# Heads of 64 divided before their transposition and multiplied in pairs; the norm sum and one split moved in the FFNs

## What is computed

```python
def rms_norm(x, g):
    return x * lax.rsqrt(jnp.mean(x * x, axis=-1, keepdims=True) + EPS) * g

# pa: 8 heads of 64, causal with a slope on the distance
logit = einsum('bhqd,bhkd->bhqk', q, k) * scale - slopes * dist
a = einsum('bhqk,bhkd->bhqd', softmax(logit), v)

# hybrid layer: three branches of width 512
# mla: 8 heads, values of 64
o_mla = einsum('bhqk,bkhd->bqhd', softmax(s), v)
# diff: 4 heads of 128 with two maps each
o_diff = einsum('bhqk,bkhd->bqhd', p[:, 0] - lam * p[:, 1], v)
# window: 8 heads of 64, two key/value heads, a sink in the denominator
m = maximum(max(s, axis=-1, keepdims=True), sink)
e = exp(s - m)
p = e / (sum(e, axis=-1, keepdims=True) + exp(sink - m))
o_win = einsum('bhgqk,bkhd->bqhgd', p, v)
merged = gates[0] * (o_mla @ w_branch[0]) + gates[1] * (o_diff @ w_branch[1]) \
       + gates[2] * (o_win @ w_branch[2])

# causal FFN
u, g = split(causal_dwconv(rms_norm(x) @ w_in), 2)
x = x + (gelu(g) * u) @ w_out
# gated FFN
x = x + (gelu(depthwise_conv(h @ w_ffn_gate)) * (h @ w_ffn_up)) @ w_ffn_down
```

## Time and profile before

| | us |
|---|---|
| median of 3 executions | 1570.9 |
| lowest, highest | 1570.85, 1575.32 |
| profiled execution | 1571.56 |
| its span in the profile | 1569.7 |
| TensorE busy | 1541.5 |
| VectorE busy | 1144.7 |
| ScalarE busy | 910.6 |
| GpSimd busy | 156.7 |

### The profile page before, as it was taken

One profiled execution on the slowest core, in us unless ns is written; L12 is line 12 of the kernel. 1 busy time (PEld: TensorE's weight loads), 2 busy tenths in 40 slices (PEclk: granted clock), 3 DMA queues, 4 the chain that ended last, 5 costly groups with the idle time before them and its releaser, 6 DMA issues.

```text
span 1569.7 us, 30181 instructions
## 1 busy us (share of the span) xinstructions
PE 1541.5 (98%) x12792; PEld 1494.6 (95%) x12792; DVE 1144.7 (73%) x1382; ACT 910.6 (58%) x1213; POOL 156.7 (10%) x91
## 2 busy tenths in 40 slices
PE   7999999999999999999999999999999999999998
PEld 7899999999999999899899999999889899999998
DVE  6768777888988787778458875678778647776666
ACT  6566544698666565556465644456645555644444
POOL 0211211100011110000030100010000013011010
PEclk9999999999999999999999999999999999999999
DMA  9345555444546545423244555544542334455552
GB/s 317 126 146 184 198 191 181 164 167 150 180 166 214 187 161 200 150 97 119 85 165 162 188 190 185 188 162 162 183 140 91 120 99 160 173 200 202 176 187 77
DMA packets 38412, 258.73 MB, mean 165 GB/s; under 512 B 4768, under 2 KB 5408, under 8 KB 7840
## 3 DMA queue, kind: packets, MB, share of 16 engines
q1 hardware_dynamic: 37872, 255.33, 46.9%
q10 hardware_dynamic: 432, 1.84, 0.3%
HBM read 256.10 MB, written 1.05 MB: 164 GB/s over the span
## 4 chain that ended last, share of the span: by engine, by line
PE 79%; issue 8%; ACT 6%; DVE 5%; POOL 0%; DMA 0%; SPq 0%; POOLq 0%; ACTq 0%; DVEq 0%
PE bank L1710 24%; PE bank L1712 23%; PE bank L1711 23%; PE bank L2019 3%; PE bank L1972 3%; PE bank L1991 2%; ACT w_hi L483 2%; DVE w_lo L990 2%; PE bank L1942 1%; DVE h_lo L1005 1%; PE bank L1915 1%; ACT h_hi L503 1%; DVE qk L1106 1%; DVE x L1081 0%; POOL y_lo L1632 0%
## 5 line engine op out<-in xcount | busy, mean ns | idle before, releaser
L1710 PE MATMUL bank<-h_hi,w_hi 128*128 128x256 f32 x2640 | 751.9, 285 | 14.2 <-DVE h_lo L1005 9.4
L1711 PE MATMUL bank<-h_lo,w_hi 128*128 128x256 f32 x2640 | 742.0, 281 | 0.0
L1712 PE MATMUL bank<-h_hi,w_lo 128*128 128x256 f32 x2640 | 741.8, 281 | 0.0
L990 DVE TENSOR_TENSOR w_lo<-raw,w_hi 128x2048 fp32r<-128x2048 f32 x237 | 549.6, 2322 | 168.6 <-ACT w_hi L483 167.4
L483 ACT ACTIVATE w_hi<-raw 128x2048 fp32r<-128x2048 f32 x237 | 452.8, 1912 | 237.5 <-PE bank L1712 237.5
L1710 PEld LDWEIGHTS bank<-h_hi,w_hi 128*128 128x128 f32 x2640 | 497.7, 189 | 26.6 <-issue 20.9
L1712 PEld LDWEIGHTS bank<-h_hi,w_lo 128*128 128x128 f32 x2640 | 500.9, 190 | 0.0
L1711 PEld LDWEIGHTS bank<-h_lo,w_hi 128*128 128x128 f32 x2640 | 497.3, 188 | 0.3
L1710 PE MATMUL bank<-y_hi,w_hi 128*128 128x256 f32 x1040 | 294.4, 283 | 3.1 <-DVE y_lo L1447 1.4
L1712 PE MATMUL bank<-y_hi,w_lo 128*128 128x256 f32 x1040 | 291.6, 280 | 0.0
L1711 PE MATMUL bank<-y_lo,w_hi 128*128 128x256 f32 x1040 | 291.5, 280 | 0.0
(11 more groups left out here) (227 smaller groups left out, 1339.7 us busy)
## 6 DMA issues: line engine op xcount, KB each, us to landing
raw<-W SPq DMA_DIRECT2D x237, 1024.0 KB, 4.8
raw<-W SPq DMA_DIRECT2D x4, 512.0 KB, 7.4
wide<-RW ACTq DMA_DIRECT2D x1, 1280.0 KB, 6.9
x<-XT SPq DMA_DIRECT2D x4, 256.0 KB, 6.6
OUT<-x SPq DMA_DIRECT2D x4, 256.0 KB, 2.0
wide<-CON SPq DMA_DIRECT2D x1, 768.0 KB, 9.7
val<-PE_T ACTq DMA_DIRECT2D x2, 256.0 KB, 2.7
vec<-VEC SPq DMA_DIRECT2D x1, 390.0 KB, 4.6
```

What stands on the lines that cost most here:

```text
L990: V.tensor_tensor(w_lo[:, n0 % NW], raw[:, n0 % NRAW], w_hi[:, n0 % NW].bitcast(F32), ALU.subtract)\
L1710: T.matmul(out, w[0], a[0], start=start, stop=False, **kw)
L1711: T.matmul(out, w[0], a[1], start=False, stop=False, **kw)
L1712: return T.matmul(out, w[1], a[0], start=False, stop=stop, **kw)
```

## The change

It has three parts.

1. Heads of 64 (all of pa, the window and mla heads of hy). `divide`, new on VectorE, multiplies a map's exponentials in `lg` by the reciprocal of their sums (with the sink's term added first) and signals `norm_done`; `transposed` waits for that instead of `exp_done`. TensorE's `output_pair`, new, takes two maps at once: the values (64 columns) are stationary and 256 columns of `pt` move, one head into partitions 0 to 63 and one into 64 to 127 of the bank, so the result is already transposed. It stands at every second step, in place of `outputs` at every step. The transpositions of `ot` by TensorE and the division by VectorE's `outputs` go; ScalarE's `leave` copies the bank to its place. The window heads are taken in another order. In hy `leave(7)` stands directly behind the first sigmoid.
2. Causal FFNs: `normed` moves from behind the first unit's products to behind tile 0 of the second unit's.
3. Gated FFNs, first step: ScalarE's `after(u)` moves ahead of its activations on the products, VectorE's ahead of the wait for them and of the convolution.

```diff
-            for h in (0, 4, 1, 5, 2, 6, 3, 7):
+            for h in (0, 5, 1, 4, 2, 7, 3, 6):
...
-        TURNS = {"pa": {5: [0], 8: [1]}, "hy": {12: [0], 13: [1], 16: [2], 17: [3], 21: [4], 24: [5]}}
+        TURNS = {"pa": {}, "hy": {12: [0], 13: [1]}}
...
-                    if not late:
+                    if not late or not s0:
                         after(u, i)
...
                     ins.then_inc(sems["tu"], 1)
-                    if late:
+                    if late and s0:
                         after(u, i)
...
+            def leave(s, g):
+
+                gg = total(s, "ogroups") + g
+                act.wait_ge(sems["pv_done"], gg + 1)
+                nc.scalar.activation(ot_tiles(s, g if kind(s) == "pa" else g - 2), bank[2 + gg % 2][:], ACT.Copy)\
+                    .then_inc(sems["o_ev"], 1)
...
+                    if kind(s) == "hy" and i in (17, 21):
+                        for g in {17: (4, 5), 21: (6,)}[i]:
+                            leave(s, g)
...
                     nc.scalar.activation(g, g, ACT.Sigmoid).then_inc(sems["sig_done"], 1)
+                    if b == 0:
+                        leave(s, 7)
                     if b < 2:
                         branch_input(s, b + 2)
-                    if b == 0:
-                        turn(s, ("pair", 5))
...
-                    if not late and s0:
+                    if not late and s0 or not causal and not s0:
                         after(u, i)
 
                     dve.wait_ge(sems["tu"], done(1))
...
-                    if late or not s0:
+                    if late and s0 or causal and not s0:
                         after(u, i)
...
+            def divide(s, i):
+
+                m, a = att_maps(s)[i], 2 + i % 2
+                dve.wait_ge(sems["exp_done"], total(s, "maps") + i + 1)
+                z = sums[:, m["col"]]
+                if m["sink"] is not None:
+                    link(V.tensor_tensor(z, z, esink[:, m["sink"]], ALU.add))
+                link(V.reciprocal(rec[:, a], z))
+                for qt in range(2):
+                    p = lg[:, i % 2, qt * S:(qt + 1) * S]
+                    last = V.tensor_scalar(p, p, rec[:, a, qt:qt + 1], None, ALU.mult)
+                last.then_inc(sems["norm_done"], 1)
...
+                if kind(s) == "pa":
+                    divide(s, 0)
...
+                    if att_maps(s)[i]["w"] == 64 and att_maps(s)[i]["dist"]:
+                        divide(s, i)
                     if i + 1 < n:
                         logits(s, i + 1)
...
                     if i + 2 < n:
                         logits(s, i + 2)
+                        if att_maps(s)[i + 1]["w"] == 64:
+                            divide(s, i + 1)
+                            if not att_maps(s)[i + 2]["dist"]:
+                                divide(s, i + 2)
...
                     else:
                         first_unit(s, ba)
-                        if causal:
-                            normed(s)
...
                     column_tile(u + 1, 0, bb[:, 0:S])
-                    if not causal and s0 == 0:
+                    if s0 == 0:
                         normed(s)
-                        embedding_sum(s)
+                        if not causal:
+                            embedding_sum(s)
...
-                    pe.wait_ge(sems["exp_done"], total(s, "maps") + u[1] + 1)
+                    if att_maps(s)[u[1]]["w"] == 64:
+                        pe.wait_ge(sems["norm_done"], normed_no(s, u[1]))
+                    else:
+                        pe.wait_ge(sems["exp_done"], total(s, "maps") + u[1] + 1)
...
+            def output_pair(s, i):
...
+                output_bank(s, i)
+                output_bank(s, i + 1)
+                pe.wait_ge(sems["pt_ev"], use_no(s, ("map", i + 1)) + 1)
+                for kt in range(2):
+                    for e in (i, i + 1):
+                        m = att_maps(s)[e]
+                        a, r = m["slot"] // 2, 64 * (m["slot"] % 2)
+                        last = T.matmul(bank[2 + (total(s, "ogroups") + m["g"]) % 2][r:r + 64, a * S:(a + 1) * S],
+                                        value(m["v"], kt), pt[:, e % 2, kt * S:(kt + 1) * S],
+                                        start=kt == 0, stop=kt == 1, skip_group_check=True)
+                        if kt and ended(s, e) is not None:
+                            last.then_inc(sems["pv_done"], 1)
...
-                    if i and (kind(s) == "pa" or i < n):
+                    if i and att_maps(s)[i - 1]["w"] == 128:
                         outputs(s, i - 1)
+                    elif i and i % 2 == 0 and (kind(s) == "pa" or i < n):
+                        output_pair(s, i - 2)
...
-                                2: lambda: outputs(s, 23),
+                                2: lambda: output_pair(s, 22),
```

78 lines of the change are left out of this document (33 added, 45 removed).

## The result

The changed kernel takes 1584.2 us (median of 5 runs, 1582.7 to 1584.5). In the same comparison before has 1575.2; its first three runs, from which I predicted, had a median of 1570.9, and over all comparisons of this study before ran between 1562.8 and 1578.6. The ratio is 1.0062, 95% interval 1.0051 to 1.0072: slower by 8.0 to 11.3 us. The profiled execution of after spans 1582.4, 12.7 more than that of before. Its mean granted clock is the lowest of the five, 0.993, where the others have 0.994 to 0.997; so what follows on the clock holds for this execution, and the others lost somewhat less by it.

What follows compares the result with a forecast made beforehand. TensorE, busy 98% of the span, was taken to bound the kernel. Two hy +7.4, pa 0, ffn0 +0.3, ffn1 -1.3, hf0 and hf1 -2.2 sum to +4.2 on 1570.9: 1575.1 us, range 1566 to 1583.

Steps and rivals of the forecast that it cites:

- VectorE late for the divided maps: In each hy: TensorE waits for VectorE's divides, the longest 4.0 us at map 9, then 0.7 at map 12.
- the price of a pair: Heads of 64: two heads' value products take 0.99 us instead of 1.68, a gain of 0.69 a pair.
- the clock: In each hy: TensorE's clock falls after the 4.0 us idle at map 9, +1.3 us a layer.
- GpSimd's hold of the divides in pa: In pa: GpSimd's pooling can hold some divides; no size of its own within the 0 taken for pa.
- The pair transposition beside map 12: In each hy: TensorE waits 0.7 us at this transposition, an estimate.
- The tail: End of attention in each hy: TensorE waits 1.0 us for ScalarE's copy of the last group behind the first sigmoid.
- the 0.99 runs from start to start and so holds the way in and out: Pairs of 64 heads: the drain at a change of tiling mode is already inside 0.99 us, adding nothing.
- The transpositions: Pair transpositions that go, four in each hy and two in pa: a gain of 0.37 us each.
- rival D: ffn0, ffn1, hy, pa: more divides held and the clock falls again; +10.6 us in all, 1581.5, chance 0.20.
- pa: Attention in pa: 3.5 us saved on TensorE against eight divides of at most 0.95; 0 taken, between -3.5 and +4.1.
- ffn0, ffn1: Causal FFNs: idle moves from the norm sums to the first product onto the result; ffn0 +0.3 us, ffn1 -1.3.
- hf0, hf1: Gated FFNs: the earlier split removes TensorE's 1.02 us wait before the second unit; -2.2 us for both layers.

Runs made afterwards that it cites:

- `f_order`: The changed kernel with VectorE's order around maps 8 and 9 turned, the split last; 1581.5 us, ratio 1.0046 to before.
- `b_two`: Before with mla heads in pairs, gated FFNs' split and last-group copy moved, window groups divided before maps 16 and 17, branch inputs behind map 21's exponentials; 1580.2 us, ratio 1.0037.
- `g_nopool`: `e_att` with GpSimd's pooling in pa left out; 1576.1 us in its one run.
- `e_mla`: Before with pairs and divides for the mla heads only (maps 16 to 23); 1573.7 us, ratio 0.9993 to before.
- `e_att`: The changed kernel with the FFN edits taken back, so the attention part alone; 1588.2 us, ratio 1.0078 to before.
- `e_causal`: Before with only the causal FFNs' norm sum moved behind tile 0 of the second unit; 1574.0 us, ratio 0.9994 to before.
- `f_fill`: The changed kernel with unread matmuls filling the waits at map 9 and at ffn0's and ffn1's first product onto the result; 1581.6 us, ratio 1.0053 to before.

## Why the prediction was wrong

The measured time lies 1.2 above the range, and at 1584.2 against 1575.1 the forecast is 9.1 too low. Of that, 4.3 are the base (1570.9 where the comparison has 1575.2) and 4.8 the change (+4.2 forecast, +9.0 measured). On the profiled executions it was +4.2 forecast, +12.7 measured, +15.2 at equal pace. That last gap of 11.0 lies in pa (4.8), hy0 and hy1 (2.7), ffn0 (1.9) and ffn1 (1.5).

The mechanism of the largest term, VectorE late for the divided maps, was right. The steps that failed are three terms of the sum: the price of a pair, taken as 0.99 and measured as 1.16; the clock, for which one fall in each hy was counted and none in pa and the causal FFNs, where it fell three times; and GpSimd's hold of the divides in pa, taken as nothing and worth 1.5.

**Waits for VectorE: right.** The sums for maps 9 (4.0, measured 3.89), 12 (0.7, 0.74), 14 (0.9, 0.90) and 22 (0.7, 0.91) held, and `f_order` and `b_two` show that they are VectorE's queue and not one misplaced divide. The pair transposition beside map 12 waited 0.48 for 0.7. The tail was off: 0.4 ahead of the first branch product and about 0.2 ahead of tile 6 in place of 1.0.

**The price of a pair: wrong.** The step that failed is "the 0.99 runs from start to start and so holds the way in and out". The way in lies ahead of the first start, where I didn't look; row 41.19 of before has it. A pair costs 1.16, not 0.99, and 20 of them 3.4 more. The transpositions gave a little more than taken, 0.43 each and not 0.37, 0.6 in all. The Trainium skill, page TensorEngine Tiling (Array Packing), section Tiling Modes, Key Properties, has the rule that a change of tiling mode drains TensorE, and I set it aside as already paid. The 0.09 ahead of each pair fits it; no run separates a drain from another cost of starting a pair.

**The clock: wrong in number.** I counted a fall in each hy, 1.3 each. It fell there, and also in pa (3.4), ffn0 and ffn1 (1.7 each). Those in the FFNs were rival D with chance 0.20, and pa's had no term at all: I worked out pa's waits and never asked how long the longest of them was. It was 1.79. What a fall costs in the end depends on who is bound: 2.6 in pa, 2.1 in ffn0, 0.7 in hy. Whether it falls behind an idle of 1.7 to 2.1 differs from run to run, and why stays open; so the number of falls in any one execution is in part luck.

**pa: wrong.** 0 was taken in a range of -3.5 to +4.1. From 32 us on it is +1.6 without a fall, of which `g_nopool` gives 1.5 to GpSimd's hold; with a fall, +4.2. The hold stood in the prediction as a possibility for two divides in hy, where it hardly occurred (0.85 and 0.62 for the two multiplications), and in one clause for pa, where it did. The prediction's two figures for hy do not fit each other either: with "up to 1.0 each" for two divides, both held is +5.3 and not +4.3.

**ffn0, ffn1: right on the waits, wrong in the sum.** The idle did move to the first product onto the result (1.83 and 2.08 for "about 2"). I took the clock of ffn1 as saved; in after it was lost again. And the -1.3 would not have lasted: `e_mla`, with before's FFNs and no fall, is 1.2 ahead of before at the first product onto the result and level with it from 472 us on. Its TensorE waits there 0.22, 0.26 and 0.78 for `y_lo` and for a split, where before waits 0.46 once. The sum ended at the first wait that shrank and did not follow the chain to the stage's end.

**hf0, hf1: right**, -1.1 each.

**The base.** I took the median of three runs, 1570.9, for before's time. The medians of the later comparisons are 1571.9 to 1575.2. The profiled execution of before had ffn1 at the quicker pace, worth 2.6; whether the pace explains the other low runs is not shown. The forecast difference should have been put on a base with a spread of 4, which the two values 1570.9 and 1575.3 in the table already showed.

## What to carry to other kernels

Work moved to an engine that is 73% busy over the span can still meet it where it is full: take the stretch in which the moved work falls, add up that engine's queue there, and see whether it ends before the other engine comes; where it does not, no order of the queue helps. When a new form of matmul is priced from a neighbour's rows, read the distance from the last start ahead of it to the first start behind it. And here, on a TensorE that is busy 98% of the span, a new wait of 2 us carried a second price in clock, in some executions and not in others. A gain at the start of a long stage counts only if the engines behind it keep up to the stage's end.

## What the runs showed of the hardware

- **Clock.** Behind the idle of 3.9 at map 9 it fell in all six cases (after, `e_att` and `g_nopool`, two layers each). Behind idles of 1.7 to 2.1 it fell in some: of four kernels with the same 1.8 at map 7 of pa in one, of the six at the first product onto the result in four (after both, `e_causal` the first, `f_order` the second), of the two at map 8 in `f_order` in one. Behind the 2.2 of `b_two` it fell both times. It also fell at 660 to 668 or 1148 to 1164 in five of the kernels with no idle above 0.5 near. Why there is open. With TensorE kept busy in the long waits (`f_fill`) it fell nowhere.
- **Two paces.** 0.1157 or 0.1184 us from one weight product to the next at full granted clock, set at an idle and held for up to 170 us. It is the largest part that I could name of before's spread. What sets it was not tried.
- **Narrow float32 matmuls.** Four float32 matmuls of 256 columns take 1.02 with 64 stationary columns in two column groups, in either order of the groups; eight with 128 take 3.6 (`f_fill`), 1.8 for four. The narrow instructions start two at a time, 0.21 apart, the wide ones one at a time, 0.215 apart. A pair behind a full-width product starts 0.09 later than another such product would.
- **GpSimd and VectorE.** A multiplication of 128x256 by a column of scalars takes 0.31 alone and up to 0.93 (mean of two) beside GpSimd's additions.
